# Gate and up weights of 32 experts fetched with another row-to-partition map

## The chip, the cores and the metric

The kernel runs on one core of a Trainium2 chip. The metric is device time in microseconds (us) of one launch; lower is better. Three runs of the kernel before the change gave 893.45, 893.39 and 891.44 us (median 893.39).

## The reference, cut to what matters

One call computes two transformer blocks on 256 tokens of width 1024: an attention block with a convolutional feed-forward part, then a hybrid mixer (gated delta rule and stick-breaking attention) followed by a mixture of experts. Each token picks one of 4 groups and 2 of its 8 experts. The change concerns only the experts:

```
for gi in range(N_GROUPS):
    hid = silu(einsum("td,edf->tef", t, expert_w_gate[gi])) * einsum("td,edf->tef", t, expert_w_up[gi])
    hid = hid * combine[:, gi, :, None]
    y = y + einsum("tef,efd->td", hid, expert_w_down[gi])
```

There are 32 experts. The gate and the up weight of one expert are each 1024 x 256 float32 in HBM (a row of 256 floats is 1 KB, and the rows lie one behind the other), and the down weight is 256 x 1024 float32 (a row is 4 KB).

## The kernel before, in words

All matrices are streamed once from HBM. Up to the router the kernel loads tiles of 1 MB (128 partitions x 2048 floats) into a ring of three buffers called `raw` (helper `load`, line 559); ScalarE and VectorE split them into a high and a low part, and TensorE multiplies with them three times (lines 1745 to 1747). Most of these weights are read 256 columns at a time with row k·128 + p on partition p, so that each piece that a DMA copies is 1 KB long.

The experts come last. Their weights stay float32 and have a ring of their own: `ring`, 5 slots, each with three tiles of 1 MB. Kind 0 holds gate and up rows 0 to 511, kind 1 gate and up rows 512 to 1023, kind 2 the down weight. `expert_load` (lines 598 to 606), on SyncE's queue (SP), fills them: two DMAs of 512 KB for a tile of kind 0 or 1, line 603, one of 1 MB for kind 2, line 606. Fourteen tiles are fetched ahead while the mixer's last matrices and the router are computed. Then SP waits until the routed tokens are laid out (`s_xga`, `s_xgv`), fetches tile (4, 2), and from then on fetches the tile of expert e after a wait on the last use of the slot by expert e - 5: `s_guse` counts the uses of kinds 0 and 1, `s_duse` those of kind 2. So 82 of the 96 tiles (54 of kinds 0 and 1, 28 of kind 2) come while the experts are computed.

The feature axis (1024) is the contraction of gate and up. It is cut in 8 chunks of 128 features; which feature lies on which partition may be chosen freely if tokens and weights agree. Before the change partition p of a half holds features 4p to 4p + 3, one in each of the half's four chunks (KH = 4). `features_of_slots` (line 2202) gathers the tokens of all slots, transposed, by multiplying X_hi and X_lo with a 0/1 matrix `pick`; it is run 16 times, 2 matmuls each (line 2205), and reads every fourth column of X as the stationary operand.

`narrow` (line 2262) is the loop over the experts; it is the one taken here, as every expert has at most 64 slots. In its order TensorE does for expert e: gate_up(e) (line 2228, 16 matmuls, each recorded twice), add(e - 2) (line 2255, sums the result of e - 2 into the tokens), down(e - 1) (line 2246), and four transposes of e (lines 2237 and 2239). ScalarE, VectorE and GpSimd prepare the operands of the neighbours meanwhile.

Of the kernel before, what the change touches and what calls it, by code (L numbers as in the profile page):

```python
# [18 lines left out]
P = 128  # L19
D = 1024  # L20
# [19 lines left out]
EFF = 256  # L40
# [7 lines left out]
WIN = 64  # L48
# [35 lines left out]
def build(nc, a, out):  # L84
    with ExitStack() as ctx:
# [55 lines left out]
        PG = ctx.enter_context(nc.psum_tensor("PG", [P, 4, 512], F32))  # L141
        PM = ctx.enter_context(nc.psum_tensor("PM", [P, 4, 512], F32))
# [324 lines left out]
        KH = KD // 2  # L467
# [3 lines left out]
        ring = [[place(f"expert_w{u}{kind}", [P, GR], ring_at[i]) for kind, i in enumerate(of)] for u, of in enumerate(RING_SLOT)]  # L471
# [5 lines left out]
        pick = place("pick", [P, TT, PAIRS], 50944, F32R)  # L477
# [75 lines left out]
        @block.sync  # L553
        def _(sp):
            def load(n, src, it=0):

                if n >= R:
                    sp.wait_ge(s_lo, n - R + 1 + 6 * it)
                sp.dma_start(raw[:, n % R, :].rearrange("p (k n) -> p k n", k=src.shape[1]), src).then_inc(landed[n % R], 16)

            sp.dma_start(X[:, 0, :], a["x"][0, 0:P, :]).then_inc(s_x[0], 16)
            sp.dma_start(X[:, 1, :], a["x"][0, P:2 * P, :]).then_inc(s_x[1], 16)
            for i in range(12):
                c = D * QKV_ORDER[i][0] + 256 * QKV_ORDER[i][1]
                load(G_QKV + i, wqkv[:, :, c:c + 256])
            for i in range(4):
                load(G_WO + i, wo[:, :, 256 * i:256 * i + 256])
            load(G_FFN, wup[:, :, 0:256])
            load(G_FFN + 1, wup[:, :, FF:FF + 256])
            with sp.Fori(0, (FJ - 1) // 2 - 1) as it:  # L570
                for u in range(2):
                    n = G_FFN + 2 + 3 * u
                    j = 2 * it + 1 + u
                    load(n, wup[:, :, bass.ds(256 * j, 256)], it)
                    load(n + 1, wup[:, :, bass.ds(FF + 256 * j, 256)], it)
                    load(n + 2, wdn[:, bass.ds(2 * j - 2, 2), :], it)
            for j in (FJ - 2, FJ - 1):
                n = G_FFN + 3 * j - 1
                load(n, wup[:, :, 256 * j:256 * j + 256])
                load(n + 1, wup[:, :, FF + 256 * j:FF + 256 * j + 256])  # L580
                load(n + 2, wdn[:, 2 * j - 2:2 * j, :])
            load(G_IN - 1, wdn[:, 2 * FJ - 2:2 * FJ, :])
            for i in range(2):
                load(G_Z + i, win[:, :, IN_Z + 256 * i:IN_Z + 256 * i + 256])
            for i, tile in enumerate(DN_ORDER):
                load(G_DN + i, win[:, :, 256 * tile:256 * tile + 256])
            for i in range(6):
                load(G_SB + i, win[:, :, IN_SB + 256 * i:IN_SB + 256 * i + 256])
            for i in range(8):
                load(G_GATE + i, win[:, :, IN_GATE + 256 * i:IN_GATE + 256 * i + 256])  # L590
            for g, name in ((G_BSB, "w_branch_sb_2"), (G_BDN, "w_branch_dn_2")):
                for i in range(2):
                    load(g + i, colview(a[name][0])[:, :, 512 * i:512 * i + 512])
            for i in range(4):
                load(G_OUT + i, colview(a["w_out_2"][0])[:, :, 256 * i:256 * i + 256])
            wexp = [a[f"expert_w_{n}_2"][0].rearrange("g e r c -> (g e) r c") for n in ("gate", "up", "down")]

            def expert_load(e, kind, u):
                dst, done = ring[u][kind], in_ring[u][kind]
                if kind < 2:  # L600
                    for i in range(2):
                        src = wexp[i][bass.ds(e, 1), D // 2 * kind:D // 2 * kind + D // 2, :].rearrange("o (p k) n -> p (o k n)", k=KH)
                        sp.dma_start(dst[:, KH * EFF * i:KH * EFF * i + KH * EFF], src).then_inc(done, 16)
                else:
                    src = wexp[2][bass.ds(e, 1), :, :].rearrange("o (f p) n -> p (o f) n", p=P)
                    sp.dma_start(dst[:, :].rearrange("p (f n) -> p f n", f=2), src).then_inc(done, 16)

            sp.wait_ge(s_gran, G_OUT)
            for e, kind in ((0, 0), (0, 1), (1, 0), (1, 1), (0, 2), (2, 0), (2, 1)):
                expert_load(e, kind, e)  # L610
            sp.wait_ge(s_mlo, 4)
            for e, kind in ((1, 2), (3, 0), (3, 1), (2, 2), (4, 0)):
                expert_load(e, kind, e)
            sp.wait_ge(s_gran, G_END)
            expert_load(4, 1, 4)
            expert_load(3, 2, 3)
            sp.wait_ge(s_xga, KD // 2)
            sp.wait_ge(s_xgv, KD // 2)
            expert_load(4, 2, 4)
            for e in range(NU, NE):  # L620
                for kind in range(2):
                    sp.wait_ge(s_guse, 2 * (e - NU) + kind + 1)
                    expert_load(e, kind, e % NU)
                if e > NU:
                    sp.wait_ge(s_duse, e - NU)
                    expert_load(e - 1, 2, (e - 1) % NU)
            sp.wait_ge(s_duse, NE - NU)
            expert_load(NE - 1, 2, (NE - 1) % NU)
            for t in range(TT):
                for i in range(2):  # L630
                    sp.wait_ge(s_h, 4 * TT + 2 * t + i + 1)
                    c = slice(D // 2 * i, D // 2 * i + D // 2)
                    sp.dma_start(out[P * t:P * t + P, c], X[:, t, c]).then_inc(s_out, 16)
            sp.wait_ge(s_out, 32 * TT)
# [1099 lines left out]
        def _(pe):  # L1734
# [209 lines left out]
            for k in range(KD):  # L1944
                mm = pe.transpose(PG[:, 0, META * k:META * k + META], MT[:, P * k:P * k + P], con("ident", META, META))
            mm.then_inc(s_xT, 1)
            keep_warm(18, con("ident"), con("ident"))
            for t in range(TT):
                for k in range(KD):
                    if k % 4 == 0:  # L1950
                        pe.wait_ge(s_h, 2 * t + k // 4 + 1)
                    mm = pe.transpose(PM[:, 2 * t + k // 4, P * (k % 4):P * (k % 4) + P], X[:, t, P * k:P * k + P], con("ident"))
# [19 lines left out]
            for st in plan:  # L1972
                kind = st[0]
                if kind in ("gran", "half"):
                    n = st[1]
# [18 lines left out]
                elif kind == "ba":  # L1994
                    pe.wait_ge(s_balo, 1)
                    bank = vacant(pe, *st)
                    for k in range(KD):
                        mm = split3(bank[0:8, 0:NT], wba_hi[:, k, :], wba_lo[:, k, :], hT_hi[:, k, :], hT_lo[:, k, :], k == 0, k == KD - 1)
                    mm.then_inc(full(*st), 1)
                elif kind == "baT":  # L2000
                    consumed(pe, "ba")
                    bank = vacant(pe, *st)
                    for c, (t0, n) in enumerate(CH):
                        mm = pe.transpose(bank[0:n, 8 * c:8 * c + 8], baT[:, t0:t0 + n], con("ident", 8, 8))
# [4 lines left out]
                elif kind in ("D", "drow"):  # L2009
                    c = st[1]  # L2010
                    n = CH[c][1]
                    pe.wait_ge(s_gm, 2 * c + 1 + (kind == "drow"))
                    bank = heads(vacant(pe, *st))
                    for h in range(DN_H):
                        if kind == "D":
                            mm = pe.matmul(bank[0:n, h, 0:n], mat(dN, cN, c)[:, h, :], con("le")[0:n, 0:n], start=True, stop=True)
                        else:
                            g = dX[:, c, h, :] if c < 2 else cV[0:n, h, :]
                            mm = pe.matmul(bank[:, h, 0:n], g, con("le")[0:n, 0:n], start=True, stop=True)
                    mm.then_inc(full(*st), 1)  # L2020
                elif kind == "dcol":
                    c = st[1]
                    n = CH[c][1]
                    pe.wait_ge(s_gm, 2 * c + 2)
                    pe.matmul(vacant(pe, *st)[0:n, 0:DN_H], con("le")[0:n, 0:n], gdec[0:n, c, :], start=True, stop=True).then_inc(full(*st), 1)
                elif kind in ("G", "QK"):
                    c = st[1]
                    t0, n = CH[c]
                    pe.wait_ge(s_l2, 4 if kind == "G" else 8)
                    bank = heads(vacant(pe, *st))  # L2030
                    for h in range(DN_H):
                        k = dnT[:, 4 + h, t0:t0 + n]
                        mm = pe.matmul(bank[0:n, h, 0:n], k, k if kind == "G" else dnT[:, h, t0:t0 + n], start=True, stop=True)
                    mm.then_inc(full(*st), 1)
                elif kind in ("ktr", "vtr"):
                    c = st[1]
                    t0, n = CH[c]
# [8 lines left out]
                elif kind == "sbv":  # L2046
                    c = st[1]
                    t0, n = CH[c]
# [6 lines left out]
                elif kind in ("L0", "T"):  # L2055
                    c = st[-1]
                    n = CH[c][1]
# [143 lines left out]

            def features_of_slots(k, t):
                for i, x in enumerate((X_hi, X_lo)):
                    mine = x[:, t, D // 2 * (k // KH):D // 2 * (k // KH) + D // 2].rearrange("p (n k) -> p k n", k=KH)[:, k % KH, :]
                    mm = pe.matmul(PM[:, k % 4, :], mine, pick[:, t, :], start=t + i == 0, stop=t + i == 2)
                if t == 1:
                    mm.then_inc(s_xg, 1)

# [12 lines left out]
            def gate_up(u, x, i2, landings, last_window):  # L2221
                for kind in range(2):
                    if landings is not None:
                        pe.wait_ge(in_ring[u][kind], 32 * landings)
                    w = ring[u][kind][:, :].rearrange("p (h k n) -> p h k n", h=2, k=KH)
                    for k in range(KH):
                        for h in range(2):
                            mm = pe.matmul(PG[WIN * h:WIN * h + WIN, i2, 0:EFF], x[:, KH * kind + k, :], w[:, h, k, :],  # L2228
                                           start=kind + k == 0, stop=kind == 1 and k == KH - 1)
                    if last_window:  # L2230
                        mm.then_inc(s_guse, 1)
                if not last_window:
                    mm.then_inc(s_gw, 1)
# [117 lines left out]
```

## Time and profile before

| | us |
|---|---|
| median of three runs | 893.39 |
| profiled execution, its time | 893.45 |
| its span in the trace | 891.7 |
| TensorE busy | 849.6 (95%) |
| TensorE weight loads busy | 701.1 (79%) |
| VectorE busy | 477.2 (54%) |
| ScalarE busy | 369.7 (41%) |
| GpSimd busy | 61.2 (7%) |

The table is to be read with the order of time in mind: the span begins with the first block and ends with the experts (from about 644 us) and the last normalisation (from about 877 us). The 1.75 us between the profiled execution's time and its span lie outside the trace. "DMA share" in the views is the time that packets took, over 16 DMA engines; as packets overlap a little, it can be over 1.

### The profile page before, as it was taken

To read this page: it belongs to the slowest core of one execution; us is meant where nothing else is said; L and a number is where in the kernel's file an instruction comes from. 1 tells how busy PE (TensorE), PEld (TensorE's weight loads), DVE (VectorE), ACT (ScalarE), POOL (GpSimd) and SP (SyncE) were. 2 spreads that over 40 slices of the span, in tenths; PEclk is the share of its full clock that TensorE was granted. 3 is DMA by queue.
4 is the path that set the end of the run, shared out by engine and by line. 5 is a ranking of instruction groups with operands and counts; after the bars stand their busy time and mean duration, and the time that the engine had idled before them with its cause. 6 is when DMAs were issued, how large, how long until landed. Compare 5 with 4: busy or idle time off the path is not lost.

```text
span 891.7 us, 15827 instructions
## 1 busy us (share of the span) xinstructions
PE 849.6 (95%) x6474; PEld 701.1 (79%) x6474; DVE 477.2 (54%) x804; ACT 369.7 (41%) x559; POOL 61.2 (7%) x88
## 2 busy tenths in 40 slices
PE   6999999999999999997999999999899999999992
PEld 6999999999999979996989999989655555555551
DVE  4455758776676786576433355586622333222226
ACT  4555655544544654673535444733211111111111
POOL 0200030000000000101111000002110000000100
PEclk9999999999999999999999999999999999999997
DMA  9864463555555543452231232579399999999941
GB/s 292 276 208 142 143 151 123 173 186 186 182 187 188 190 141 96 143 154 90 88 96 51 94 96 95 180 281 408 133 398 408 408 409 408 409 408 409 409 190 49
DMA packets 102000, 193.48 MB, mean 217 GB/s; under 512 B 4461, under 2 KB 70336, under 8 KB 101808
## 3 DMA queue, kind: packets, MB, share of 16 engines
q1 hardware_dynamic: 99664, 185.61, 58.0%
q0 software_dynamic: 1696, 4.59, 1.7%
q10 hardware_dynamic: 576, 2.36, 0.8%
q8 instruction: 48, 0.79, 0.4%
q14 instruction: 16, 0.13, 0.0%
HBM read 191.50 MB, written 1.05 MB: 216 GB/s over the span
## 4 chain that ended last, share of the span: by engine, by line
PE 84%; DVE 7%; ACT 5%; issue 3%; DMA 1%; DVEq 0%; ACTq 0%
PE PG L1745 13%; PE PG L2228 13%; PE PG L1747 13%; PE PG L1746 12%; PE PG L2246 7%; PE PM L2255 4%; PE PM L2081 2%; PE PM L1745 2%; PE PM L1747 2%; PE PM L1746 2%; ACT whi L750 2%; PE PM L2146 1%; DVE wlo L1174 1%; PE PG L2237 1%; PE PG L1805 1%
## 5 line engine op out<-in xcount | busy, mean ns | idle before, releaser
L1745 PE MATMUL PG<-hT_hi,whi 128*128 128x256 f32 (+1 forms) x832 | 240.1, 289 | 0.0
L1747 PE MATMUL PG<-hT_hi,wlo 128*128 128x256 f32 (+1 forms) x832 | 235.4, 283 | 0.0
L1746 PE MATMUL PG<-hT_lo,whi 128*128 128x256 f32 (+1 forms) x832 | 235.4, 283 | 0.0
L1174 DVE TENSOR_TENSOR wlo<-raw,whi 128x2048 fp32r<-128x2048 f32 x76 | 174.1, 2291 | 90.2 <-ACT whi L750 90.2
L1745 PEld LDWEIGHTS PG<-hT_hi,whi 128*128 128x128 f32 x832 | 157.5, 189 | 5.3 <-issue 2.5
L1747 PEld LDWEIGHTS PG<-hT_hi,wlo 128*128 128x128 f32 x832 | 157.6, 189 | 0.0
L750 ACT ACTIVATE whi<-raw 128x2048 fp32r<-128x2048 f32 x76 | 145.0, 1908 | 30.0 <-PE PG L1747 27.1
L1746 PEld LDWEIGHTS PG<-hT_lo,whi 128*128 128x128 f32 x832 | 157.1, 189 | 0.3
L2228 PE MATMUL PG<-expert_w,xw 128*64 128x256 f32 x992 | 113.9, 382 | 0.0
L1684 DVE SCALAR_TENSOR_TENSOR y_lo<-PG,small,y_hi 128x512 fp32r<-128x512 f32 x32 | 24.0, 751 | 160.2 <-ACT y_hi L1121 160.2
L2228 PEld LDWEIGHTS PG<-expert_w,xw 128*64 128x64 f32 x992 | 68.5, 137 | 36.5 <-issue 5.2
L2246 PE MATMUL PG<-expert_w,hid 128*64 128x512 f32 x256 | 61.9, 604 | 0.0
L1121 ACT ACTIVATE y_hi<-PG,small 128x512 fp32r<-128x512 f32 x32 | 22.0, 688 | 85.9 <-PE PG L2246 85.9
L1115 ACT ACTIVATE gusum<-PG 128x256 f32<-128x256 f32 x32 | 12.3, 385 | 106.2 <-PE PG L2228 106.2
L2246 PEld LDWEIGHTS PG<-expert_w,hid 128*64 128x64 f32 x256 | 15.6, 136 | 29.8 <-issue 29.6
L1745 PE MATMUL PG<-whi,hT_hi 128*128 128x256 f32 x128 | 36.4, 284 | 1.3 <-DVE hT_lo L1430 0.9
L1747 PE MATMUL PG<-whi,hT_lo 128*128 128x256 f32 x128 | 36.0, 281 | 0.0
L1746 PE MATMUL PG<-wlo,hT_hi 128*128 128x256 f32 x128 | 35.9, 281 | 0.0
L719 POOL COPY xw<-pair 128x512 f32 x31 | 19.1, 617 | 207.8 <-PE PG L2228 189.2
L1805 PE MATMUL PG<-cst 128*128 128x128 f32 (+1 forms) x166 | 28.0, 327 | 4.8 <-DMA cst<-in_consts 4.8
L1745 PE MATMUL PM<-whi,hid_hi 128*128 128x512 f32 x80 | 31.7, 396 | 0.2 <-DVE wlo L1174 0.2
L2255 PE MATMUL PM<-y_hi,hot 64*128 64x512 f32 x128 | 28.8, 444 | 2.9 <-DVE y_lo L1684 2.9
(443 smaller groups left out, 1329.5 us busy)
## 6 DMA issues: line engine op xcount, KB each, us to landing
expert_w<-in_expert_w_gate SPq DMA_DIRECT2D x64, 512.0 KB, 13.7
expert_w<-in_expert_w_up SPq DMA_DIRECT2D x64, 512.0 KB, 15.1
expert_w<-in_expert_w_down SPq DMA_DIRECT2D x32, 1024.0 KB, 15.9
raw<-in_ffn_w_up SPq DMA_DIRECT2D x22, 1024.0 KB, 5.1
raw<-in_w_in SPq DMA_DIRECT2D x22, 1024.0 KB, 5.2
raw<-in_moba_w_qkv SPq DMA_DIRECT2D x12, 1024.0 KB, 6.2
raw<-in_ffn_w_down SPq DMA_DIRECT2D x11, 1024.0 KB, 4.9
raw<-in_moba_w_o SPq DMA_DIRECT2D x4, 1024.0 KB, 5.1
```

The lines of the kernel that those rows point to most:

```text
L719: pool.tensor_copy(xw[i2][:, :, :], pair[:, :, bass.ds(at, WIN)]).then_inc(s_win, 1)
L750: act.activation(hi_of(n), raw[:, n % R, :], ACT.Copy).then_inc(s_hi, 1)
L1121: act.activation(y_hi[:, :], result, ACT.Copy, scale=slotw[i2]).then_inc(s_yhi, 1)
L1174: dve.tensor_tensor(lo_of(n), raw[:, n % R, :], hi_of(n).bitcast(F32), ALU.subtract).then_inc(s_lo, 1)
L1684: dve.scalar_tensor_tensor(y_lo[:, :], result, slotw[i2], y_hi[:, :].bitcast(F32), ALU.mult, ALU.subtract).then_inc(s_y, 1)
L1745: pe.matmul(dst, lh, rh, start=start, stop=False, **kw)
L1746: pe.matmul(dst, lh, rl, start=False, stop=False, **kw)
L1747: return pe.matmul(dst, ll, rh, start=False, stop=stop, **kw)
L1805: pe.matmul((PG[:, 3, :] if bank is None else bank)[:, 0:x.shape[1]], w, x, start=True, stop=True)
L2228: mm = pe.matmul(PG[WIN * h:WIN * h + WIN, i2, 0:EFF], x[:, KH * kind + k, :], w[:, h, k, :], start=kind + k == 0, stop=kind == 1 and k == ...
L2246: mm = pe.matmul(result[WIN * h:WIN * h + WIN, :], hid2[i2][:, f, :], w[:, f, 512 * h:512 * h + 512], start=f == 0, stop=f == 1)
L2255: mm = pe.matmul(PM[:, 2 * t + h, :], hot[i2][x, P * t:P * t + P], y[x, :], start=first and y is y_hi, stop=last and y is y_lo)
```

## The change

Gate and up rows are dealt to the partitions in another way. Before, partition p of a half holds the 4 successive rows 4p to 4p + 3, which are 4 KB in one piece both in HBM and in the tile. After, it holds rows p, 128 + p, 256 + p and 384 + p, which are four pieces of 1 KB, in HBM and in the tile, where gate and up of one row now lie side by side. The number of DMAs, their bytes, their waits, and the tiles' sizes and places stay. The down weight's load is not touched. `features_of_slots` reads 128 successive columns of X in place of every fourth one, and gate_up takes its moving operand from the new place.

```diff
                 if kind < 2:
                     for i in range(2):
-                        src = wexp[i][bass.ds(e, 1), D // 2 * kind:D // 2 * kind + D // 2, :].rearrange("o (p k) n -> p (o k n)", k=KH)
-                        sp.dma_start(dst[:, KH * EFF * i:KH * EFF * i + KH * EFF], src).then_inc(done, 16)
+                        src = wexp[i][bass.ds(e, 1), D // 2 * kind:D // 2 * kind + D // 2, :].rearrange("o (k p) n -> p (o k) n", p=P)
+                        sp.dma_start(dst[:, :].rearrange("p (k n) -> p k n", k=KH)[:, :, EFF * i:EFF * i + EFF], src).then_inc(done, 16)
...
             def features_of_slots(k, t):
                 for i, x in enumerate((X_hi, X_lo)):
-                    mine = x[:, t, D // 2 * (k // KH):D // 2 * (k // KH) + D // 2].rearrange("p (n k) -> p k n", k=KH)[:, k % KH, :]
-                    mm = pe.matmul(PM[:, k % 4, :], mine, pick[:, t, :], start=t + i == 0, stop=t + i == 2)
+                    mm = pe.matmul(PM[:, k % 4, :], x[:, t, P * k:P * k + P], pick[:, t, :], start=t + i == 0, stop=t + i == 2)
...
-                    w = ring[u][kind][:, :].rearrange("p (h k n) -> p h k n", h=2, k=KH)
+                    w = ring[u][kind][:, :].rearrange("p (k n) -> p k n", k=KH)
                     for k in range(KH):
                         for h in range(2):
-                            mm = pe.matmul(PG[WIN * h:WIN * h + WIN, i2, 0:EFF], x[:, KH * kind + k, :], w[:, h, k, :],
+                            mm = pe.matmul(PG[WIN * h:WIN * h + WIN, i2, 0:EFF], x[:, KH * kind + k, :], w[:, k, EFF * h:EFF * h + EFF],
                                            start=kind + k == 0, stop=kind == 1 and k == KH - 1)
```

## Rows read from the trace of the kernel before

**Rows 1.** The page: 40 equal slices of the span, DMA share and rate.
```profile
DMA  9864463555555543452231232579399999999941
GB/s 292 276 208 142 143 151 123 173 186 186 182 187 188 190 141 96 143 154 90 88 96 51 94 96 95 180 281 408 133 398 408 408 409 408 409 408 409 409 190 49
```

**Rows 2.** The chain of waits in order of time: start us, us, what.
```profile
827.46 3.60 PE PG L2228 x32
831.06 1.13 PE PM L2255 x8
832.19 1.87 PE PG L2246 x8
834.65 3.60 PE PG L2228 x32
...
863.44 3.60 PE PG L2228 x32
...
876.60 0.75 PE PM L2255 x4
```

**Rows 3.** By stretch: us; PE, PEld, DVE, ACT, POOL busy; PE clock; DMA share; GB/s.
```profile
632.00:643.00 11.00, 9.53 (x37) 8.16 (x35) 6.61 (x18) 2.40 (x4) 0.00 (x0) 1.00 0.00 0
660.00:680.00 20.00, 20.00 (x150) 10.55 (x146) 6.37 (x18) 3.34 (x8) 1.23 (x2) 1.00 1.02 408
```

**Rows 4.** DMA from 660 to 850 us: all packets, then the queue of SyncE.
```profile
DMA packets 20878, 77.66 MB, mean 409 GB/s; under 512 B 1960, under 2 KB 1960, under 8 KB 20862
...
q1 hardware_dynamic: 20862, 77.43, 102.2%
```

**Rows 5.** DMA issues from 839 to 840 us: KB each, us from issue to landing.
```profile
expert_w<-in_expert_w_up SPq DMA_DIRECT2D x1, 512.0 KB, 15.8
```

**Rows 6.** SyncE's queue in order of time, 838 to 842 us.
```profile
839.17 1.09 SPq L603 DMA_DIRECT2D expert_w<-in_expert_w_up  x1
```

**Rows 7.** DMA from 10 to 15.5 us: all packets, then the queue of SyncE.
```profile
DMA packets 1894, 1.92 MB, mean 349 GB/s; under 512 B 22, under 2 KB 1894, under 8 KB 1894
...
q1 hardware_dynamic: 1894, 1.92, 110.2%
```

**Rows 8.** By stretch, while tiles of `raw` land in pieces of 1 KB (columns: Rows 3).
```profile
4.00:8.00 4.00, 2.08 (x8) 1.78 (x8) 0.22 (x2) 2.07 (x4) 0.00 (x0) 1.00 1.00 323
...
102.00:103.50 1.50, 1.50 (x18) 1.02 (x18) 0.72 (x5) 1.50 (x2) 0.00 (x0) 1.00 1.09 383
309.00:310.00 1.00, 1.00 (x11) 1.00 (x10) 0.59 (x2) 1.00 (x3) 0.00 (x0) 1.00 1.08 384
317.00:319.00 2.00, 1.72 (x8) 1.09 (x7) 0.69 (x1) 1.41 (x2) 0.00 (x0) 1.00 1.09 348
```

**Rows 9.** SyncE's queue in order of time, 8 to 16 us.
```profile
2.89 5.13 SPq L559 DMA_DIRECT2D raw<-in_moba_w_qkv  x1
```

**Rows 10.** TensorE in order of time: line 2205, then lines 1745 to 1747.
```profile
639.83 0.39 PE L2205 MATMUL PM<-pick,X_hi 128*128 128x512 f32 x1
...
642.88 0.40 PE L2205 MATMUL PM<-pick,X_lo 128*128 128x512 f32 x1
...
211.67 0.39 PE L1746 MATMUL PM<-wlo,hid_hi 128*128 128x512 f32 x1
...
213.94 0.39 PE L1747 MATMUL PM<-whi,hid_lo 128*128 128x512 f32 x1
```

**Rows 11.** Line 2205's weight loads (ns min/median/max), and a group's (busy us, mean ns).
```profile
L2205 PEld LDWEIGHTS PM<-pick,X_hi x16: 308/309/312, 635.4 to 642.4; 128*128 128x128 f32 x16
...
L1746 PEld LDWEIGHTS PG<-hT_lo,whi 128*128 128x128 f32 x832 | 157.1, 189 | 0.3
```

**Rows 12.** By stretch, as TensorE comes to rest (columns: Rows 3).
```profile
860.00:880.00 20.00, 14.88 (x96) 7.06 (x94) 6.46 (x13) 4.34 (x8) 0.00 (x0) 0.97 0.01 2
```

## The prediction

> **What bounds the kernel now.** I read three views, the slices first. From the 28th slice to the 38th DMA moves 398 to 409 GB/s at a share of 9 tenths or more, except in one slice at 133 GB/s; before that the rate lies under 300 [rows 1]. So the experts are the only long part in which the DMA engines have no reserve, and they are also the part whose loads the diff edits.
>
> The chain of waits says who sets the time there. From one gate_up to the next 834.65 - 827.46 = 7.19 us pass, made of 3.60 (line 2228), 1.13 (line 2255), 1.87 (line 2246) and 0.59 for the transposes and hand-overs between; all of it is TensorE, and no DMA is in the chain [rows 2]. The table by stretch has TensorE busy 20.00 of 20 us and DMA share 1.02 at once [rows 3]. TensorE sets the pace, but the transfers are close behind, in fact a little slower: a tile of 1 MB (1.0486 MB) at 409 GB/s takes 2.564 us [rows 4], three of them 7.69 us, 0.50 more than the 7.19 of TensorE. What hides this is the prefetch. The DMA engines stand still from 632 to 643 us [rows 3] with 14 tiles in the ring, and the lead shrinks by 0.5 us with each expert, as long as new loads come.
>
> How much lead is left at the end is the number on which everything hangs. The last load of kinds 0 and 1 (the up half of expert 31) is issued at 839.17 [rows 6] and lands 15.8 us later [rows 5], at 855.0. gate_up(31) starts at 863.44 [rows 2]; its second half, which reads that tile, starts 3.60 / 2 = 1.8 later, at 865.2. The lead is 865.2 - 855.0 = 10.2 us. From this half to the last matmul (876.60 + 0.75 = 877.35) it is 12.15 us [rows 2], whatever the loads do.
>
> **The change part by part.**
>
> **Loads, line 603.** DMAs, bytes and waits stay; only the pieces change, from 4 KB to four of 1 KB. While experts are computed, 54 tiles of kinds 0 and 1 come and 28 of kind 2; the latter keep 2.564 us. The price of a 1 KB piece is the one unknown, and the first blocks show it, since they read `raw` in such pieces. From 10 to 15.5 us only SyncE's queue runs, every engine full (share 110.2%), 1894 packets under 2 KB: 349 GB/s [rows 7]. A tile then takes 1.0486 / 0.349 = 3.005 us, 0.441 more. But there are better stretches: 383 and 384 GB/s where one tile lands by itself, and 348 again when a second tile follows at once [rows 8]. At 384 a tile takes 2.731, or 0.167 more. And there is a worse one: 323 GB/s from 4 to 8 us, with a share of 1.00 [rows 8], in which constants come by ScalarE's queue too; there a tile is 3.246, 0.682 more. I take 349. It is the longest stretch with this kind of packet alone, and it is a backlog, as the experts are; 383 and 384 are seen only in single tiles. The sum: 54 x 0.441 = 23.8 us (bounds 54 x 0.167 = 9.0 and 54 x 0.682 = 36.8).
>
> Of this the lead hides 10.2, and 13.6 stay. The first experts see nothing. A round of three tiles becomes 2 x 3.005 + 2.564 = 8.57 us against 7.19, so the lead falls by 1.38 per expert and runs out some 13.6 / 1.38 = 10 experts before the end, near expert 22. From there each gate_up waits for its tile. Behind this wait stand, on TensorE, add and down of the two experts before, which delays the vectors by as much; SP's next loads wait for the uses of the ring too, but the transfers have some four experts' tiles on order by then, so no hole opens there.
>
> **The prefetch.** 10 of its 14 tiles are of kinds 0 and 1: 10 x 0.441 = 4.4 us more. They lie before 632 us, and 11 us of DMA rest follow [rows 3]; they cost nothing as long as a tile takes less than 1.1 us more. The loads of `raw` are ahead of them in the same queue.
>
> **SP's queue.** Four times as many pieces fill the queue sooner. Already an issue of a 1 KB tile was held for 5.13 us at the start, behind two others of its kind [rows 9]. SP will be held more often, but it has nothing else to issue until the output, after the last matmul, and a held issue means that the engines have work. I put it at 0; if pieces are also made more slowly than they are moved, that is in the 323 bound.
>
> **features_of_slots, line 2205.** 32 matmuls. From the first row shown to the last there are 13 steps in 3.05 us, 0.235 each; lines 1745 to 1747 with the same 512 columns and stationary operands in successive columns need 2.27 / 10 = 0.227 [rows 10]. So 32 x 0.008 = 0.2 to 0.3 us go, on the path, and the ring's last part starts earlier by the same: I take 0.2. The weight load itself takes 309 ns with every fourth column and 189 without [rows 11], but it lies under the matmul before it; were all 120 ns on the path the gain would be 3.8 us, which the steps of 0.235 exclude.
>
> **gate_up's moving operand, line 2228.** A row of 256 floats stays in one piece; only the distance to the next changes. 0, with no row that speaks for another value.
>
> **Sum.** 893.45 (the profiled execution) + 23.8 - 10.2 - 0.2 = 906.8 us. The execution is the slowest of the three runs and 0.06 over their median, so the same holds for the median.
>
> **A rule of the Trainium skill weighed.** The row: the same engines move 409 GB/s in pieces of 4 KB and 349 in pieces of 1 KB, 15% less [rows 4, 7]. The Trainium skill, page "DMA: Bandwidth & Descriptors", section Specifications, gives 512 B as the smallest transfer for line rate, and its section "Why small descriptors are slow" an overhead of about 3 cycles a packet, which is an estimate of (32 + 3) cycles for 1 KB against (128 + 3) for 4 KB, 7% less. By the first the change costs nothing; by the second a tile takes about 2.74 us, again under the point where it begins to cost. This trace disagrees with the first and, in the backlog, with the second as well. The sum above doesn't use either.
>
> **The rivals.**
>
> *The lead hides it all (not slower).* The place is the same tile of expert 31, and the price decides: the extra is hidden as long as 54 times it stays under 10.2 + 0.2 = 10.4, that is 0.193 us a tile, or 1.0486 / 2.757 = 380 GB/s. For it speak 383 and 384 [rows 8], and that the expert rows lie one behind the other in HBM, while those of `raw` are cut from longer rows. Against it: the second tile of a burst falls to 348, and a backlog is what the experts have. TensorE then remains the bound, and only the 0.2 us of line 2205 show: 893.2 us. The page's figures above lead here.
>
> *A mixed backlog is worse.* Rows 8 have 323 GB/s while several queues ran. If making the pieces for DMAs already in the queue holds the engines, this is also the rate of the experts: 36.8 - 10.4 = 26.4, 919.9 us. Against it: with 4 KB pieces SP's issues in this stage are held as well (1.09 us at 839.17 [rows 6]), and the rate stays 409.
>
> *The weight loads were a bound.* If the steps of line 2205 fall to less than the 0.227 of rows 10, or the earlier start reaches further, something like 1 us is won and the loads stay hidden: 892.4 us. This needs both a rate over 380 and a step no row shows.
>
> **How the numbers follow.** The forecast (340 to 365 GB/s) has 0.60, hidden 0.15, worse than 340 0.22, faster 0.03. Its own range: 365 GB/s gives 2.873 us a tile, 54 x 0.309 - 10.4 = 6.3, 899.7; 340 gives 3.084, 54 x 0.520 - 10.4 = 17.7, 911.1. The range for 8 in 10 goes from 893 (part of the hidden case) to 918 (most of the worse one). Within 0.3% (2.7 us) is about what a measurement of this kernel can't tell from no change. Cases of sign: slower 0.82, same 0.15, faster 0.03. TensorE's clock adds little: it was granted at 0.97 where TensorE is at rest for 5 of 20 us [rows 12]; a fall of that size over the last 12 us is 0.4.
>
> **What would show it.** In the profile after: the rate in the 28th and later slices falls from 409 to about 3.146 MB / 8.57 us = 367 GB/s, at a share still near 1.05; the step from gate_up to gate_up is 7.19 until about expert 22 and then 8.6; idle TensorE before line 2228 ended by a DMA of expert_w, some 13 us in total; weight loads of line 2205 near 189 ns. I am wrong if the rate of the 1 KB tiles is over 380 (no wait for DMA appears), or if waits appear in the first ten experts, which would mean that the rate is far lower or that SP's queue runs dry.

## The result and the profile after

The changed kernel takes 907.12 us (median of four runs, 906.05 to 909.07) against 893.42: the ratio is 1.0158, 95% interval 1.0135 to 1.0183. It is slower by 13.7 us; 906.8 was forecast.

The slices of the page of the changed kernel, which answer to [rows 1]: DMA share in tenths and the rate.

```profile
DMA  9854454555555624442312324499699999999991
GB/s 292 287 186 140 153 136 141 186 185 185 185 185 186 208 73 139 139 144 91 94 48 94 94 93 140 138 334 370 203 365 365 368 363 368 367 365 369 366 351 49
```

The experts' slices are as full as before, but show 363 to 370 GB/s in place of 398 to 409. The first half, which reads 1 KB pieces in both kernels, shows no such fall (185 to 186 GB/s in slices 9 to 13, 182 to 188 before). Between 660 and 850 us (answers to [rows 4]), all packets and then SyncE's queue:

```profile
DMA packets 52576, 69.63 MB, mean 366 GB/s; under 512 B 1764, under 2 KB 46899, under 8 KB 52561
...
q1 hardware_dynamic: 52561, 69.42, 107.3%
```

Of 52,576 packets 46,899 are now under 2 KB; before it were 1960. The forecast mixture was 367 GB/s. The rate of [rows 7], 10 to 15.5 us, is 349 GB/s in this profile too.

The chain of waits in order of time (start us, us, what) answers to [rows 2]. Through the experts it is TensorE (and 0.39 us of ScalarE in expert 0) until 781 us, and from then on it goes through transfers of the up weights and the queue that issues them:

```profile
770.44 3.60 PE PG L2227 x32
...
777.64 3.63 PE PG L2227 x32
781.27 1.73 SPq L603
...
868.87 9.91 DMA expert_w<-in_expert_w_up
...
878.83 1.95 PE PG L2227 x16
...
890.33 0.75 PE PM L2254 x4
```

The row at 868.87 is the up half of expert 31. It is issued there, lands 9.9 us later at 878.8, and the second half of gate_up(31) starts at 878.83 (line 2227 is line 2228 of the kernel before). In the kernel before the tile landed at 855.0 and was used at 865.2. TensorE's waits, by line (us in total, times, longest us), from 640 us to the end:

```profile
PE PG L2227 <- DMA expert_w<-in_expert_w_up: 9.9, 15, 1.0
PE PM L2254 <- DVE y_lo L1684: 2.9, 2, 1.8
```

The first such wait is in the second half of expert 22 (TensorE in order of time: start us, us, operation, and in brackets idle us and its releaser). From there all ten experts wait before their second half, and five of them for a shorter time before the first half too, which makes the 15. The step between experts is 867.33 - 858.74 = 8.59 us:

```profile
799.16 1.95 PE L2227 MATMUL PG<-expert_w,xw 128*64 128x256 f32 x16
801.66 1.95 PE L2227 MATMUL PG<-expert_w,xw 128*64 128x256 f32 x16 [0.55 <-DMA expert_w<-in_expert_w_up]
...
858.74 1.95 PE L2227 MATMUL PG<-expert_w,xw 128*64 128x256 f32 x16
861.63 1.95 PE L2227 MATMUL PG<-expert_w,xw 128*64 128x256 f32 x16 [0.95 <-DMA expert_w<-in_expert_w_up]
...
867.33 1.95 PE L2227 MATMUL PG<-expert_w,xw 128*64 128x256 f32 x16 [0.17 <-DMA expert_w<-in_expert_w_up]
```

The idle time in brackets is counted from the modelled end of the matmul before, so its sum of 9.9 us is less than the loss. The loss itself is best read as the length of the experts' stage, from the first matmul of gate_up(0) to the end of the last of line 2255 (2254 after). Before it is 644.11 to 877.79 (877.36 + 0.43), 233.68 us. After it is 644.64 to 891.52 (891.10 + 0.42), 246.88 us: 13.20 more. What is left of the 13.7 lies within the spread of what comes before the experts: the stage starts between 641.5 and 646.7 us in the profiles of this study, in kernels that hardly differ there. So the stage length is compared below beside the times. It is steady where the times are not: the four profiles with no wait for a DMA give 233.67 to 233.69 us.

### The profile page after: what moved, and what is told of

It reads as the page before. It is cut to its first block, busy times and chain, and to the rows that moved or that the text cites. A ratio compares the mean times of both kernels' runs of the same rounds, so it can differ in the third digit from the quotient of the medians.

```text
span 905.4 us, 15827 instructions
## 1 busy us (share of the span) xinstructions
PE 853.0 (94%) x6474; PEld 701.3 (77%) x6474; DVE 477.0 (53%) x804; ACT 369.4 (41%) x559; POOL 61.2 (7%) x88
## 4 chain that ended last, share of the span: by engine, by line
PE 74%; DVE 7%; SPq 7%; ACT 5%; DMA 4%; issue 3%; ACTq 0%; DVEq 0%
PE PG L1745 13%; PE PG L1747 12%; PE PG L1746 12%; PE PG L2227 9%; SPq L603 5%; PE PG L2245 4%; DMA expert_w<-in_expert_w_up 3%; PE PM L2254 2%; PE PM L2081 2%; PE PM L1745 2%; PE PM L1747 2%; PE PM L1746 2%; ACT whi L750 2%; SPq L606 2%; PE PM L2146 1%
## 5 line engine op out<-in xcount | busy, mean ns | idle before, releaser
L2227 PE MATMUL PG<-expert_w,xw 128*64 128x256 f32 x992 | 116.1, 383 | 10.4 <-DMA expert_w<-in_expert_w_up 9.9
L2245 PE MATMUL PG<-expert_w,hid 128*64 128x512 f32 x256 | 61.9, 604 | 0.0
## 6 DMA issues: line engine op xcount, KB each, us to landing
expert_w<-in_expert_w_down SPq DMA_DIRECT2D x32, 1024.0 KB, 10.6
```

What stands on the lines that cost most here:

```text
L2245: mm = pe.matmul(result[WIN * h:WIN * h + WIN, :], hid2[i2][:, f, :], w[:, f, 512 * h:512 * h + 512], start=f == 0, stop=f == 1)
```

## The experiments

Seven more kernels were run. "Stage" is the length just defined, read from one profile of each. Each ratio is to the kernel before timed beside it: its median is 893.42 us beside the changed kernel, 894.34 beside the next four rows' kernels and 894.31 beside the last three.

| kernel | pieces of kinds 0 and 1 | us | ratio, 95% interval | stage, us | against 233.68 |
|---|---|---|---|---|---|
| changed kernel | 1 KB, both sides | 907.12 | 1.0158 (1.0135 to 1.0183) | 246.88 | +13.20 |
| dst_pieces | 4 KB in HBM, 1 KB in SBUF | 906.73 | 1.0137 (1.0117 to 1.0157) | 247.13 | +13.45 |
| src_pieces | 1 KB in HBM, 4 KB in SBUF | 906.20 | 1.0135 (1.0115 to 1.0156) | 247.10 | +13.42 |
| one_kind | kind 0 1 KB, kind 1 4 KB | 894.75 | 1.0012 (1.0000 to 1.0024) | 235.13 | +1.45 |
| two_kb | 2 KB, both sides | 893.60 | 0.9987 (0.9973 to 1.0001) | 233.68 | 0.00 |
| half_kb | 4 KB in HBM, 512 B in SBUF | 948.34 | 1.0605 (1.0588 to 1.0623) | 289.32 | +55.64 |
| gather_only | 4 KB, as before | 892.92 | 0.9993 (0.9980 to 1.0007) | 233.69 | +0.01 |
| less_down | 1 KB, half the down weights' bytes | 894.07 | 1.0003 (0.9991 to 1.0015) | 233.67 | -0.01 |

**dst_pieces and src_pieces: which side makes a piece short.** The first is the kernel before with

```diff
-....rearrange("o (p k) n -> p (o k n)", k=KH)
-sp.dma_start(dst[:, KH * EFF * i:KH * EFF * i + KH * EFF], src)
+....rearrange("o (p k) n -> p (o k) n", k=KH)
+sp.dma_start(dst[:, :].rearrange("p (k n) -> p k n", k=KH)[:, :, EFF * i:EFF * i + EFF], src)
```

and gate_up's operand as in the changed kernel (the cuts here leave out `.then_inc`, which stays). The second is the changed kernel with

```diff
-sp.dma_start(dst[:, :].rearrange("p (k n) -> p k n", k=KH)[:, :, EFF * i:EFF * i + EFF], src)
+sp.dma_start(dst[:, :].rearrange("p (h k n) -> p h k n", h=2, k=KH)[:, i, :, :], src)
```

and gate_up's operand as before.

> Rows 4p to 4p + 3 stay on partition p as before (4 KB in one piece in HBM), and line 2205 is as before; only the tile has gate and up of one row side by side, so that the pieces are 1 KB on the SBUF side alone. Theory (the length of a piece decides, whichever side cuts it): a tile takes 3.005 us as in the changed kernel, TensorE waits for expert_w from about expert 22, 907 us. Rival (scattered reads of HBM decide): 409 GB/s, no wait, 893.4 us. Rival in between (both sides count): 895 to 904 us.

> Rows p, 128 + p, ... as in the changed kernel (1 KB pieces in HBM), line 2205 as in the changed kernel, but the tile keeps gate and up apart, 4 KB in one piece in SBUF. Theory (the shorter side's length decides): as the changed kernel, 907 us, rate 366 GB/s while experts run. Rival (the write side decides): 409 GB/s, 893.2 us.

Both take what the changed kernel takes, within 1 us. DMA from 680 to 850 us in dst_pieces:

```profile
DMA packets 46926, 62.33 MB, mean 367 GB/s; under 512 B 1575, under 2 KB 41800, under 8 KB 46913
```

The rows are read from HBM in one run of 4 KB and still the packets are under 2 KB and the rate is 367 GB/s. So the order of the reads in HBM costs nothing here, and a cut on one side is a cut of the transfer. What counts is the longest run that is whole on both sides.

**one_kind: does the lead add up as said.** Kind 0 is loaded, and its four chunks gathered, as in the changed kernel, kind 1 as before:

```diff
+                        if kind == 0:
+                            src = src.rearrange("o (k p) n -> p (o k) n", p=P)
+                            sp.dma_start(dst[:, :].rearrange("p (k n) -> p k n", k=KH)[:, :, EFF * i:EFF * i + EFF], src).then_inc(done, 16)
+                        else:
+                            src = src.rearrange("o (p k) n -> p (o k n)", k=KH)
+                            sp.dma_start(dst[:, KH * EFF * i:KH * EFF * i + KH * EFF], src).then_inc(done, 16)
```

> Only tiles of kind 0 are fetched in 1 KB pieces; kind 1 stays at 4 KB, and line 2205 is changed for the first four chunks alone. Theory (the extra adds up against a lead of 10.2 us at the last tile of kind 1): 27 x 0.441 = 11.9 us more, 10.2 hidden, 0.1 won at line 2205: 1.6 more, 895.0 us, waits only in the last one or two experts. Rival (each late tile costs, in proportion, no lead): half of the changed kernel's 13.7 us, 900.3 us.

The stage is 1.45 us longer, not half of 13.2. The times agree, but say less by themselves: the ratio's interval runs from 0 to 2.1 us. TensorE in order of time, experts 30 and 31, the only ones with a wait:

```profile
857.64 1.95 PE L2235 MATMUL PG<-expert_w,xw 128*64 128x256 f32 x16 [0.30 <-DMA expert_w<-in_expert_w_up]
863.30 1.95 PE L2235 MATMUL PG<-expert_w,xw 128*64 128x256 f32 x16
865.76 1.95 PE L2235 MATMUL PG<-expert_w,xw 128*64 128x256 f32 x16 [0.52 <-DMA expert_w<-in_expert_w_up]
```

DMA from 700 to 840 us runs at 387 GB/s, and a cut tile of 3.005 us beside two of 2.564 gives 3.146 / 8.133 = 387. Half of the extra transfer time costs a ninth of the loss. This is what a threshold looks like, and the threshold is where the lead of 10.2 us had put it.

**two_kb: the price of a piece.** Two successive rows on a partition, in the tile gate pair beside up pair; line 2205 reads every second column, and gate_up's operand follows.

```diff
-....rearrange("o (k p) n -> p (o k) n", p=P)
-sp.dma_start(dst[:, :].rearrange("p (k n) -> p k n", k=KH)[:, :, EFF * i:EFF * i + EFF], src)
+....rearrange("o (k p j) n -> p (o k) (j n)", p=P, j=2)
+sp.dma_start(dst[:, :].rearrange("p (k n) -> p k n", k=2)[:, :, 2 * EFF * i:2 * EFF * i + 2 * EFF], src)
```

> Tiles of kinds 0 and 1 in pieces of 2 KB on both sides (two successive rows on a partition), line 2205 reads every second column. Theory (a piece costs a fixed time and a time by its bytes): per engine 4 KB takes 160.2 ns at 409 GB/s and 1 KB 46.9 ns at 349, so 9.1 ns and 36.9 ns per 1000 bytes; 2 KB is 84.7 ns, 387 GB/s, a tile 2.71 us, 54 x 0.147 = 7.9 us more, less than the lead of 10.2: no wait for a DMA, 893.3 us, and the up half of expert 31 lands 2 to 3 us ahead of its use. Rival (all that is cut falls to 349): 907 us. Rival (2 KB costs nothing): 893.3 us too, but with 409 GB/s in the expert part and the lead still 10.

DMA from 700 to 840 us:

```profile
DMA packets 23689, 55.14 MB, mean 394 GB/s; under 512 B 1395, under 2 KB 1395, under 8 KB 23679
```

A round of three tiles with 2.711 us for the cut ones is 3.146 MB / (2 x 2.711 + 2.564) = 394 GB/s, which is the rate measured; it is not the 409 of uncut pieces. The extra is real and hidden. The last up half is issued at 851.10 and takes 12.7 us to land:

```profile
expert_w<-in_expert_w_up SPq DMA_DIRECT2D x1, 512.0 KB, 12.7
```

so it is there at 863.8, and gate_up(31) (at 864.15 in the chain) uses it 1.8 us after its start, at 865.95. Of the lead of 10.2 us 2.1 are left.

**half_kb: below 1 KB.** Rows, HBM side and line 2205 as before; 128 columns of gate and 128 of up alternate in the tile, so gate_up's operand is two runs of 128 columns. That costs TensorE nothing: before the first wait the step between experts is 7.19 us, as in the kernel before.

```diff
-....rearrange("o (p k) n -> p (o k n)", k=KH)
-sp.dma_start(dst[:, KH * EFF * i:KH * EFF * i + KH * EFF], src)
+....rearrange("o (p k) (c n) -> p (o k c) n", k=KH, c=2)
+sp.dma_start(dst[:, :].rearrange("p (q n) -> p q n", q=2 * KH)[:, :, P * i:P * i + P], src)
```

> Rows 4p to 4p + 3 on partition p and line 2205 as before, but a tile of kinds 0 and 1 has 128 columns of gate beside 128 of up, so that the pieces are 512 B on the SBUF side. Theory (9.1 ns a piece and 36.9 ns per 1000 bytes, from the rates at 4 KB and 1 KB): 28.0 ns, 293 GB/s, a tile 3.58 us, 54 x 1.02 = 54.9 us more, 10.2 hidden: 938 us, and TensorE waits from about expert 9 (round of three tiles 9.72 us against 7.19). Rival (no cost from 512 B up): 893.4. Rival (the cost below 1 KB grows faster than the two terms say): over 945.

The stage is 55.6 us longer, 11 more than the two terms gave, so the last rival holds, in a mild form. The table by stretch (us; PE, PEld, DVE, ACT, POOL busy; granted clock; DMA share; GB/s), before the waits and while TensorE waits:

```profile
660.00:680.00 20.00, 20.00 (x152) 10.75 (x149) 6.37 (x18) 3.72 (x9) 1.23 (x2) 1.00 1.08 311
...
740.00:915.00 175.00, 129.40 (x887) 67.05 (x885) 36.09 (x102) 21.06 (x51) 9.83 (x16) 0.99 1.04 305
```

From 660 to 740 us as a whole it is 315 GB/s, at a share of 1.10. At 311 to 315 GB/s three tiles take 10.11 to 9.99 us, so a cut tile takes 3.77 to 3.71 us and a piece 29.5 to 29.0 ns, not 28.0. With that, 54 x (3.77 - 2.564) - 10.2 = 54.9 us, and 51.7 with 3.71; the loss is 55.6. What is missing comes while TensorE waits: from expert 14 to expert 31 (741.33 and 916.77 us) the step is 175.44 / 17 = 10.32 us, which is 305 GB/s, and the DMA share is 1.04 in place of 1.10, down to 0.96 from 820 to 840 us. So the engines were no longer full all the time. It fits that SP's loads wait for slots which a late TensorE frees late, but no run separates this.

The first wait is at expert 14 (741.33), not 9. The forecast's own terms say so too: its 44.7 us of lateness at 9.72 - 7.19 = 2.53 us per expert are 17.7 experts before the end. The count was wrong, not the terms.

**gather_only: line 2205 alone.** The kernel before with

```diff
-                    mine = x[:, t, D // 2 * (k // KH):D // 2 * (k // KH) + D // 2].rearrange("p (n k) -> p k n", k=KH)[:, k % KH, :]
-                    mm = pe.matmul(PM[:, k % 4, :], mine, pick[:, t, :], start=t + i == 0, stop=t + i == 2)
+                    mm = pe.matmul(PM[:, k % 4, :], x[:, t, P * k:P * k + P], pick[:, t, :], start=t + i == 0, stop=t + i == 2)
```

> Only line 2205 is changed (successive columns of X); the weights stay as before, so tokens and weights no longer agree in their features and the experts' part of the output is another. Theory: steps of line 2205 0.227 in place of 0.235 us, weight loads 189 in place of 309 ns, 0.2 us won, no wait for a DMA, 893.2 us, which a median can't tell from the kernel before. Rival (the weight load was on the path): 1 to 3.8 us won, 889.6 to 892.4.

The ratio can't be told from 1, but the trace can tell (line 2204 here; first and last of the 32 matmuls, then gate_up(0)):

```profile
633.50 0.47 PE L2204 MATMUL PM<-pick,X_hi 128*128 128x512 f32 x1 [1.48 <-DVE pick L1660]
...
640.63 0.39 PE L2204 MATMUL PM<-pick,X_lo 128*128 128x512 f32 x1
641.85 3.67 PE L2227 MATMUL PG<-expert_w,pair 128*64 128x256 f32 x32 [0.83 <-issue]
```

From the first of them to gate_up(0) it is 8.35 us, the same as in the changed kernel (636.29 to 644.64); in the kernel before it is 8.71 (635.40 to 644.11). The weight loads have a median of 188 ns in place of 309. The gain is 0.36 us.

**less_down: take the transfer time away.** The changed kernel, with

```diff
+                    part = D if isinstance(e, int) and e < NU else D // 2
-                    src = wexp[2][bass.ds(e, 1), :, :].rearrange("o (f p) n -> p (o f) n", p=P)
-                    sp.dma_start(dst[:, :].rearrange("p (f n) -> p f n", f=2), src)
+                    src = wexp[2][bass.ds(e, 1), :, 0:part].rearrange("o (f p) n -> p (o f) n", p=P)
+                    sp.dma_start(dst[:, :].rearrange("p (f n) -> p f n", f=2)[:, :, 0:part], src)
```

> The changed kernel, but of the down weights of experts 5 to 31 only the left 512 columns are loaded (half of the bytes; the products with the right half are computed with what the slot held, so the output is another). Pieces of 2 KB for those, 1 KB for kinds 0 and 1 as in the changed kernel. Theory (the transfers' total time against the lead is all that costs): 27 tiles take about 1.36 in place of 2.564 us (524 KB at 387 GB/s), 32.5 us less than in the changed kernel against 13.6 of lateness: no wait for a DMA, 893.2 us. Rival (1 KB pieces or the held issues of SP cost by themselves, whatever the load on the engines): 900 to 907.

No wait for a DMA is left and the stage is back at 233.67 us, with 1 KB pieces at the same price: 2.621 MB / (2 x 3.005 + 1.36) = 356 GB/s. DMA from 700 to 840 us:

```profile
DMA packets 45133, 49.77 MB, mean 355 GB/s; under 512 B 1515, under 2 KB 40279, under 8 KB 45123
...
q1 hardware_dynamic: 45123, 49.62, 108.5%
```

355 GB/s is the lowest rate of all kernels with pieces of 1 KB or more, and it costs nothing. The number of pieces is that of the changed kernel (only those of the down weights are half as long), and they come faster: 45,133 in 140 us are 322 per us, against 52,576 in 190 us, 277 per us. So it was not the making of the pieces that set the 366 GB/s of the changed kernel. Neither the piece nor the full queue hurts by itself; only the transfers' sum against the lead does.

## Why the prediction was right, step by step

**The price of a tile.** 349 GB/s from 10 to 15.5 us of the kernel before was the right row among four: a step between experts of 8.59 us against 8.57 forecast, and 366 GB/s against 367. The 383 and 384 GB/s of single tiles would have led to "no change". That a backlog, not the first tile of a burst, is the state of the experts was argued from what the stage does, and the stage bore it out. Why the single tile is faster was not tried and stays open.

**The lead.** 10.2 us from one landing and one use. The runs around it hold it from both sides: 7.9 us of extra is hidden (two_kb) with 2.1 left, 11.9 leaves 1.45 (one_kind), 23.8 leaves 13.20. These three give a lead between 10.0 and 10.6. The fourth, half_kb, agrees roughly and no more: at 311 GB/s its extra is 65.1 us and leaves 55.6, a lead of 9.5, but at 315 it would be 61.9 and the lead 6.3.

**The sum.** 13.6 us were to stay in the stage and 13.20 did. The first wait came at expert 22, as forecast. That the total came out at 907.12 against 906.8 is closer than the terms are, and in part luck: 893.45 + 13.20 - 0.36 is 906.3, and the kernel before alone ran from 891.2 to 896.3 us in the 19 runs beside the last experiments, with a median of 894.3.

**Line 2205.** 0.36 us won, 0.2 forecast. The steps themselves went from 0.235 to 0.227, as forecast (7.05 and 6.82 us for the last 30 of them), so the rival in which the weight loads were a bound did not occur. What was short is that the rows left out the first step: from the first matmul to the last it is 7.48 us before and 7.13 after, and the first step, 0.43 before and 0.31 after, gives 0.12 of that. The weight loads became 120 ns shorter, and nearly all of it was hidden, as the steps had said.

**The prefetch.** In the changed kernel the last prefetched bytes come between 636 and 638 us (DMA share 0.13 in that stretch, 0.00 from 638 to 643), so it was hidden. In the kernel before they had come by 632 us; 4.4 us later was forecast, and it is 4 to 6.

**SP's queue.** Priced at 0, which less_down shows. But one sentence there was wrong in its size: "some four experts' tiles on order". The up half of expert 31 is issued 9.9 us before it lands, 9.9 / 8.59 = 1.2 experts' transfers; before it was 15.8 us, 2.1 experts'. SP waits less for the ring's slots (from 660 to 880 us 17 times, 20.8 us, in place of 52 times, 77.5 us) and is held more at its issues, and the page's chain names it for 7% of the span. That reads like a new bound, and isn't one: with fewer bytes and as many issues the loss is gone (less_down). The conclusion drawn from the four experts' tiles, that no hole opens, held all the same with 1 KB pieces (DMA share 1.07 and 1.08 from 780 to 860 us); in half_kb it fell to 0.96.

**The rival "the lead hides it all"** fell with the rate, not with its mechanism: two_kb and less_down are that rival, come true at 387 GB/s a cut tile and at fewer bytes. **The "mixed backlog"** at 323 GB/s did not occur at 1 KB. As for the rules weighed, the Trainium skill ("DMA: Bandwidth & Descriptors", Specifications, and "Why small descriptors are slow") would have given no change by either rule (the second by an estimate of 2.74 us a tile); with pieces of 1 KB and of 512 B the measured cost is larger than both.

## What to carry to other kernels

Where TensorE sets the pace and the DMA engines are full beside it, look up how far ahead the last load lands: that lead is a budget. The extra time of all loads adds up against it; it costs nothing up to the lead and its full amount past it. Price transfers by a stretch in the same state (a backlog, one kind of packet), not by the best stretch of the trace. When a layout is changed to make one engine's reading simpler, keep the longest run whole on both sides of the DMA; here 0.36 us was won on TensorE and 13 lost on the engines that feed it.

## What the runs showed of the hardware

- A piece's time on one of the 16 engines, in a backlog: 160 ns for 4 KB (409 GB/s), about 85 for 2 KB (the rate that fits 394 in the mixture), 46.9 for 1 KB (349), 29.0 to 29.5 for 512 B (283 to 278). These are estimates from the rates shown. From 4 KB to 1 KB this is 9.1 ns and 36.9 ns per 1000 bytes; the line goes through these two, the 2 KB run falls on it, and at 512 B it is 1.0 to 1.5 ns too low. The same 1 KB pieces move at 383 and 384 GB/s where one tile lands by itself [rows 8]; the cause of that difference is open.
- A cut on the SBUF side alone, with runs of 4 KB in HBM, costs as much as a cut on the HBM side (stages of 247.13 and 247.10 us).
- The chain of waits can name the queue that issues (SPq; 7% of the span here) where the transfers are what is late. The test is whether the stage shortens when bytes go and the number of issues stays; it did.
